# First FFN product by one level of Strassen's algorithm over 1024-token halves

## The reference

```python
    x = layer_norm(DEEPNORM_ALPHA * x + merged @ w_o, ln1_g, ln1_b)
    gate, up = jnp.split(x @ w_ffn_in, 2, axis=-1)          # (2048,1024) @ (1024, 2*2816)
    ffn = (jax.nn.silu(gate) * up) @ w_ffn_out              # (2048,2816) @ (2816,1024)
    return layer_norm(DEEPNORM_ALPHA * x + ffn, ln2_g, ln2_b)
```

## Time and profile before

| | |
|---|---|
| median of 3 runs | 1044.1 us |
| the profiled execution's own time | 1043.92 us |
| its span on the slowest core (6) | 1042.4 us |
| spans of the other cores | 1031.3 to 1039.8 us |
| TensorE busy | 1000.3 us (96%) |
| VectorE, ScalarE, GpSimd busy | 407.6, 328.0, 159.9 us |
| HBM read, written | 147.17 MB, 22.08 MB |
| mean granted TensorE clock, core 6 | 0.990 |

### The profile page before, as it was taken

The page is one execution under the profiler, slowest core; times in us unless marked ns, Lnnn a source line. Parts: engine busy times, 40 slices in busy tenths (PEclk is TensorE's granted clock), DMA queues, the critical chain, the costliest instruction groups (busy, mean ns, idle before and its releaser), DMA issues.

```text
span 1042.4 us, 15773 instructions; the slowest of 8 cores (1031.3 to 1042.4 us)
## 1 busy us (share of the span) xinstructions
PE 1000.3 (96%) x5782; PEld 466.5 (45%) x5782; DVE 407.6 (39%) x745; ACT 328.0 (31%) x472; POOL 159.9 (15%) x214
## 2 busy tenths in 40 slices
PE   4999999978999999999999999999999999999995
PEld 1455544533444444444444444444444444444442
DVE  0324576657562222222268652342124321332124
ACT  0135665746452222222225642011111111111110
POOL 3200000202244333333401320010001000000001
PEclk9999999989899999999999999999999999999998
DMA  9995145645259999800193786134421544144301
GB/s 136 176 173 103 23 91 107 82 91 78 47 83 134 139 193 141 129 1 2 46 235 134 174 220 202 41 121 149 155 81 61 177 147 142 41 141 146 117 22 60
DMA packets 40971, 118.37 MB, mean 114 GB/s; under 512 B 5120, under 2 KB 17032, under 8 KB 39648
## 3 DMA queue, kind: packets, MB, share of 16 engines
q0 software_dynamic: 13408, 49.55, 29.2%
q1 hardware_dynamic: 27488, 67.81, 22.0%
HBM read 147.17 MB, written 22.08 MB: 162 GB/s over the span
## 4 chain that ended last, share of the span: by engine, by line
PE 90%; DMA 5%; issue 1%; DVE 1%; ACT 1%; SPq 0%; POOL 0%; DVEq 0%; ACTq 0%; POOLq 0%
PE ps L231 89%; DMA arena<-w_out 2%; DMA arena<-u_scratch 2%; DMA arena<-w_glu 1%; PE ps L1068 1%; SPq L146 0%; DVE arena L1018 0%; ACT arena L595 0%; PE ps L686 0%; POOL arena L146 0%; ACT arena L643 0%; PE ps L758 0%; ACT arena L722 0%; DVE arena L1020 0%; PE ps L569 0%
## 5 line engine op out<-in xcount | busy, mean ns | idle before, releaser
L231 PE MATMUL ps<-arena 128*128 128x512 bf16 (+5 forms) x5372 | 983.5, 363 | 28.4 <-DMA arena<-xt 12.6
L231 PEld LDWEIGHTS ps<-arena 128*128 128x128 bf16 (+2 forms) x5372 | 446.4, 98 | 549.1 <-issue 71.0
L1106 DVE TENSOR_TENSOR arena<-ps,arena 128x512 bf16<-128x512 f32 x88 | 60.3, 690 | 202.4 <-PE ps L231 190.2
L827 DVE SCALAR_TENSOR_TENSOR arena<-arena,ps 128x512 f32<-128x512 f32 x96 | 65.8, 686 | 148.7 <-PE ps L231 144.7
L806 ACT ACTIVATE arena<-ps,bgate_sb 128x512 f32<-128x512 f32 x96 | 65.8, 686 | 163.3 <-PE ps L231 163.3
L1104 ACT ACTIVATE arena<-ps 128x512 f32<-128x512 f32 x88 | 52.1, 596 | 194.2 <-PE ps L231 194.2
L998 ACT ACTIVATE arena<-arena 128x1024 bf16<-128x1024 f32 (+1 forms) x32 | 33.8, 1055 | 157.7 <-DVE arena L1127 148.0
L1013 POOL TENSOR_TENSOR mvt<-mvt,eps_t 128x1 f32<-128x1 f32 x32 | 20.9, 653 | 394.9 <-DVE mvt L1008 394.8
L834 POOL TENSOR_TENSOR arena<-arena 128x512 f32<-128x512 f32 x32 | 40.7, 1273 | 123.3 <-DVE arena L827 123.3
L643 ACT ACTIVATE arena<-ps 128x1024 bf16<-128x1024 f32 x46 | 46.6, 1024 | 12.2 <-PE ps L231 11.9
L839 POOL TENSOR_TENSOR arena<-arena 128x512 bf16<-128x512 f32 x32 | 41.2, 1289 | 43.2 <-DVE arena L827 41.7
(11 more groups left out here) (90 smaller groups left out, 316.1 us busy)
## 6 DMA issues: line engine op xcount, KB each, us to landing
arena<-w_bf_cache SPq DMA_DIRECT2D x88, 512.0 KB, 3.5
arena<-u_scratch SPq DMA_DIRECT2D x64, 135.0 KB, 4.3
arena<-x SPq DMA_DIRECT2D x16, 512.0 KB, 29.5
out<-arena POOLq DMA_DIRECT2D x16, 512.0 KB, 2.9
arena<-w_f POOLq DMA_DIRECT2D x22, 256.0 KB, 7.9
arena<-w_g POOLq DMA_DIRECT2D x9, 512.0 KB, 18.9
arena<-xt POOLq DMA_DIRECT2D x8, 512.0 KB, 31.7
w_bf_cache<-w_f POOLq DMA_DIRECT2D x8, 512.0 KB, 6.2
```

The costliest lines, as they stand in the source:

```text
L231: return pe.run(lambda: nc.tensor.matmul(out, lhsT, rhs, start=start, stop=stop), deps, inc)
L827: t_y = dve.run(lambda: nc.vector.scalar_tensor_tensor(out=gb[r], in0=gb[r], scalar=1.0, in1=ps[:, bk, :], op0=ALU.add, op1=ALU.mult), [tk ...
L1106: t_a = dve.run(lambda: nc.vector.tensor_tensor(out=actT[:, j, :], in0=ps[:, bU, :], in1=sgf[sr], op=ALU.mult), [tU, t_s, e_state["dep"]])
```

## The change

`w_ffn_in` is seen as two blocks of 512 rows by 22 pairs of 128-column blocks, the input as halves of 1024 tokens, each two blocks of 512 tokens by two blocks of 512 features. Each 2x2 block product is then made with seven products in place of eight.

- *Weight forms.* Seven sums or plain blocks of the weights per unit. `fold_load`, `fold_sum` and its store make them in stage C: a load of 512 KB from the bf16 copy, three VectorE additions, a store of 896 KB to a new DRAM tensor, on SP's queue, two buffers. `straight` calls a fold after every sixth item of columns 1 to 3 (eight each, 22 in all).
- *Input forms.* `e_sums` makes five differences of x1T blocks on VectorE, at the start of each half.
- *The unit.* `f1_unit` makes four 128x512 results (two column blocks by two token blocks) of the gate or of the up part: 28 matmuls in four banks. Three products are copied out to SBUF (ScalarE), summed by GpSimd, and the later products accumulate onto the same banks; VectorE then combines bank and copy. Silu and multiply follow; two of each are put off into the next unit (`late`).
- *x and x1.* x is loaded into 12 buffers at the end of column 3, none at the start of column 1; x1 is stored to DRAM after LayerNorm 1 and loaded again for the second product (`load_hb`). `w2` takes over the buffers of x1, its 22 loads come from unit 7 on.
- *Order.* Twelve `d_chain` calls lie among the w_o blocks, eight among the units (after units 0, 1, 3, 4, 6, 7, 9, 10). The FFN goes in two halves of 1024 tokens: 11 gate units and 11 up units in turn, then eight blocks of the second product.

```diff
+    def fold_load(v):
+        if v < 22:
+            fold_ld[v] = dma(sp, FG[v % 2][:, 0:4], w1b_d[v], fg_slot[v % 2], [w1_raw[v], fold_st.get(v - 2), a_done])
...
+    def fold_sum(v):
+        G = FG[v % 2].rearrange("p s k c -> p s (k c)")
+
+        def twice(sl):
+            return bass.AP(G.tensor, G[:, sl, 0:1].offset, [[G.ap[0][0], 128], [0, 2], [1, 512]])
+
+        dve.run(lambda: nc.vector.tensor_tensor(out=G[:, 4:6, :], in0=G[:, 0:2, :], in1=twice(3), op=ALU.add), [fold_ld[v]])
+        dve.run(lambda: nc.vector.tensor_tensor(out=G[:, 6:8, :], in0=G[:, 0:2, :], in1=twice(2), op=ALU.add))
+        t = dve.run(lambda: nc.vector.tensor_tensor(out=G[:, 8, :], in0=G[:, 3, :], in1=G[:, 2, :], op=ALU.subtract))
+        fold_st[v] = dma(sp, w1f_d[v], FG[v % 2][:, 2:9], fs_slot[v % 2], [t])
+
+    fold_n = iter(range(22))
+
+    def fold_step():
+        v = next(fold_n, None)
+        if v is not None:
+            fold_load(v + 1)
+            fold_sum(v)
...
+    def straight(items, each=0):
+        for i, (_, f) in enumerate(items):
             f()
             tick()
+            if each and i % each == each - 1:
+                fold_step()
 
...
-        load_x(tb, [a_done])
     t_ln1 = load(ln1t, bass.AP(ln1_d.tensor, 0, [[0, 128], [D, 2], [1, D]]), [a_done, t_sT[3, 3]], sp)
+    fold_load(0)
     load_wg(2, [pe.tok()])
     load_wos(2, [])
     cache_w1(4)
-    straight(cat([c_main(1, tt) for tt in range(4)]))
+    straight(cat([c_main(1, tt) for tt in range(4)]), 6)
...
     load_wg(3, [pe.tok()])
     load_wos(3, [])
     t_wo = load(w_o_sb, w_o_d, [a_done])
     cache_w1(3)
-    straight(cat([c_main(2, tt) for tt in range(4)]))
+    straight(cat([c_main(2, tt) for tt in range(4)]), 6)
     dp2_done = pe.tok()
     w1_tok = {}
     s_w2 = new_slot("w2")
-    e_state = {"sgi": 0, "oi": 0}
...
+    def load_w2(j):
+        w2_tok[j] = load(w2[j], w_f2_d[:, j, :], [x1_st[j // 2 + (12 if j < 8 else 0)]])
...
+    def load_w1(u):
+        if u < 44:
+            r = u % 3
+            w1_tok[u] = dma(sp, w1s[r], w1f_d[u % 22], w1_slot[r], [w1_free[r], fold_st[u % 22]])
...
+    straight(cat([c_main(3, tt) for tt in range(4)]), 6)
     c_done = pe.tok()
-    w1_free[2] = [c_done]
...
+    def load_x(tb):
+        t_x[tb] = dma(sp, X1[tb % 12], x_d[tb * 128:(tb + 1) * 128, :], x_slot[tb % 12], x1_free.get(tb - 12, [c_done]))
+
+    for tb in range(12):
+        load_x(tb)
+        if tb in (7, 9):
+            load_w1((tb - 7) // 2)
+    x1b_free = [[g_done], [g_done], [g_done]]
...
         d_state["ln"] = t_ln
+        x1_st[tb] = dma(sp, x1_d[tb * 128:(tb + 1) * 128, :], xb, st_slot[tb % 12], [t_ln])
+        x1_free[tb] = [x1_st[tb], d_state["cb", tb]]
+        if tb + 12 < 16:
+            load_x(tb + 12)
...
+    def e_sums(P, deps):
+        q = x1T[:, P].rearrange("p h k t -> p (h k t)")
...
+        t = [t_x1T[8 * P:8 * P + 8], fold_st[20], fold_st[21], deps]
+        sa_tok[P, 4] = dve.run(lambda: nc.vector.tensor_tensor(
+            out=S[:, 4:5, :], in0=quarter(3), in1=quarter(0), op=ALU.subtract), t)
+        sa_tok[P, 2] = dve.run(lambda: nc.vector.tensor_tensor(
+            out=S[:, 2:4, :], in0=quarter(1, 2), in1=twice(0), op=ALU.subtract))
+        sa_tok[P, 0] = dve.run(lambda: nc.vector.tensor_tensor(
+            out=S[:, 0:2, :], in0=quarter(1, 2), in1=twice(3), op=ALU.subtract))
+
+    tg_free = [[c_done], [c_done]]
+    tu_free = [[]]
+    late = {"act": [], "pool": []}
...
+    def f1_unit(u):
+        P, v = u // 22, u % 22
+        i, up = v // 2, v % 2
+        n = (v // 2) % 2
+        load_w1(u + 2)
+        W = w1s[u % 3]
+        A11, A22 = x1T[:, P, 0, 0:4, :], x1T[:, P, 1, 4:8, :]
+        T3, T4, T1 = TU if up else TG[n][0:3]
+        t_free = tu_free[0] if up else tg_free[n]
+        (ba, da), (bb, db), (bc, dc), (bd, dd) = [banks.alloc(1) for _ in range(4)]
+
+        def prod(b, form, rhs, first, deps):
+            for kc in range(4):
+                tk = mm(ps[:, b, :], W[:, form, kc, :], rhs[:, kc, :], first and kc == 0, kc == 3,
+                        deps if kc == 0 else (), inc=(kc == 3), onto=not first)
+            return tk
+
+        def grab(dst, b, deps):
+            return act.run(lambda: nc.scalar.copy(dst, ps[:, b, :]), deps)
+
+        tM3 = prod(ba, 2, A11, True, [da, w1_tok[u], t_x1T[8 * P:8 * P + 8]])
+        t3 = grab(T3, ba, [tM3, t_free, sa_tok[P, 0]])
+        run_late("act")
+        tM4 = prod(bb, 5, A22, True, [db])
+        t4 = grab(T4, bb, [tM4])
+        s = pool.run(lambda: nc.gpsimd.tensor_tensor(out=T3, in0=T3, in1=T4, op=ALU.add), [t3, t4])
+        run_late("act")
+        tM1 = prod(bc, 6, SA[:, 4], True, [dc, sa_tok[P, 4]])
+        t1 = grab(T1, bc, [tM1])
+        s1 = pool.run(lambda: nc.gpsimd.tensor_tensor(out=T1, in0=T3, in1=T1, op=ALU.add), [s, t1])
+        run_late("pool", 2)
+        tM6 = prod(bd, 4, SA[:, 3], True, [dd, sa_tok[P, 2]])
+        tM5 = prod(ba, 1, SA[:, 2], False, [t3])
+        tM2 = prod(bb, 0, SA[:, 1], False, [t4, sa_tok[P, 0]])
+        tM7 = prod(bc, 3, SA[:, 0], False, [t1])
+        w1_free[u % 3] = [tM7]
+        e_state["mm"] = tM7
+
+        def dsub(dst, b, deps, op):
+            return dve.run(lambda: nc.vector.tensor_tensor(out=dst, in0=dst, in1=ps[:, b, :], op=op), deps)
+
+        g = dsub(T3, ba, [tM5, s1], ALU.subtract)
+        if not up:
+            N = TG[n][3]
+            sg12 = act.run(lambda: nc.scalar.activation(T4, ps[:, ba, :], AF.Silu), [g])
+            banks.release(ba, sg12)
+            h = dsub(T1, bb, [tM2], ALU.subtract)
+            sg21 = act.run(lambda: nc.scalar.activation(N, ps[:, bb, :], AF.Silu), [h])
+            banks.release(bb, sg21)
+        else:
+            sg12, sg21, sg22, sg11 = e_state["sg"]
+            G3, G4, G1, GN = TG[n]
+            j1, j2 = actT[2 * i], actT[2 * i + 1]
+            a_tok[2 * i + 1, 0] = dve.run(lambda: nc.vector.tensor_tensor(
+                out=j2[:, 0:512], in0=ps[:, ba, :], in1=G4, op=ALU.mult), [sg12, g, e_state["dep"]])
+            banks.release(ba, a_tok[2 * i + 1, 0])
+            h = dsub(T1, bb, [tM2], ALU.subtract)
+            a_tok[2 * i, 1] = dve.run(lambda: nc.vector.tensor_tensor(
+                out=j1[:, 512:1024], in0=ps[:, bb, :], in1=GN, op=ALU.mult), [sg21, h])
+            banks.release(bb, a_tok[2 * i, 1])
+        c22 = dsub(T1, bd, [tM6, h], ALU.add)
+        banks.release(bd, c22)
+        c11 = dsub(T3, bc, [tM7, g], ALU.add)
+        banks.release(bc, c11)
+        if not up:
+            e_state["sg"] = [sg12, sg21, None, None]
+            sg = e_state["sg"]
+
+            def silu22():
+                sg[2] = act.run(lambda: nc.scalar.activation(T1, T1, AF.Silu), [c22])
+
+            def silu11():
+                sg[3] = act.run(lambda: nc.scalar.activation(T3, T3, AF.Silu), [c11])
+            late["act"] += [silu22, silu11]
+        else:
+            sg = e_state["sg"]
+
+            def mul22():
+                a_tok[2 * i + 1, 1] = pool.run(lambda: nc.gpsimd.tensor_tensor(
+                    out=j2[:, 512:1024], in0=T1, in1=G1, op=ALU.mult), [c22, sg[2], e_state["dep"]])
+
+            def mul11():
+                a_tok[2 * i, 0] = pool.run(lambda: nc.gpsimd.tensor_tensor(
+                    out=j1[:, 0:512], in0=T3, in1=G3, op=ALU.mult), [c11, sg[3]])
+                tg_free[n] = [a_tok[2 * i, 0], a_tok[2 * i, 1]]
+                tu_free[0] = [a_tok[2 * i, 0]]
+            late["pool"] += [mul11, mul22] if v == 21 else [mul22, mul11]
+
...
+    def load_hb(tb):
+        if tb < 16:
+            r = tb % 3
+            hb_tok[tb] = dma(sp, HB[r], x1_d[tb * 128:(tb + 1) * 128, :], hb_slot[r], [x1_st[tb], hb_free[r]])
...
         d_mm(tb)
         d_H(tb)
-        if tb >= 2 and tb % 3:
+        if tb >= 2 and tb not in (5, 10):
             d_chain()
     e_start()
-    si = 0
...
-        e_step(si)
+    e_sums(0, [c_done])
+    w2_order = list(range(8, 22)) + list(range(8))
+    for u in range(22):
+        f1_unit(u)
+        if u % 3 != 2 and chain["k"] < 18:
+            d_chain()
...
+        if u >= 7:
+            for _ in range(2):
+                if w2_order:
+                    load_w2(w2_order.pop(0))
...
+    for P in range(2):
+        run_late("act", 2)
+        run_late("pool", 2)
+        if P == 0:
+            e_sums(1, [e_state["mm"]])
+            for tb in range(3):
+                load_hb(tb)
+        for tb in range(8 * P, 8 * P + 8):
+            f2_block(tb)
+        if P == 0:
+            for u in range(22, 44):
+                f1_unit(u)
     pool.wait([s.tok() for s in s_out])
     return nc, {e.name: set(e.needed) for e in engines}
 
...
```

More of the change, by code:

```diff
@@ L228, in bank2, with mm @@
         return ps[:, b:b + 2, :].rearrange("p a b -> p (a b)")
-    def mm(out, lhsT, rhs, start, stop, deps=(), inc=False):
-        return pe.run(lambda: nc.tensor.matmul(out, lhsT, rhs, start=start, stop=stop), deps, inc)
```

(53 more changed lines are left out.)

155 lines of the change are left out of this document (49 added, 106 removed).

## The result

The changed kernel takes 1133.0 us (median of 4 runs, 1130.9 to 1134.8), the kernel before 1043.0 us in the runs beside it: a ratio of 1.086, 95% interval 1.083 to 1.089. The forecast was 1126 us. All eight cores are slower by about the same (spans of 1117.6 to 1129.4 us; the stops in stage C add up to 64.0 to 68.0 us on each), so one core stands for the others.

The account below looks back on a forecast made before the run. TensorE, busy 96% of the span, was taken to bound the kernel. 1043.9 - 38.0 (matmuls) + 65 (stage C) + 8 (clock) + 9 (first unit) + 30 (chains) + 8 (turns) = 1125.9, forecast 1126 us; range 1050 to 1160.

Parts of the forecast that it names:

- Matmuls, -38.0: First FFN product: 1232 matmuls in place of 1408, 176 fewer at 0.2158 us each, saving 38.0 us.
- Stage C, 65: Merge stage: VectorE's waits for fold loads stop TensorE for 29 and 16 us in column 1, 20 in column 2.
- the walk: Step-by-step reckoning of when loads, stores and engines finish; in stage C, fold load 0 about 371 us, TensorE resuming at 374.
- w_o stage and first unit, 9: LN chains on VectorE, then e_sums and evacuations, delay the first unit's end from 578.1 to 587.4 us: 9 us.
- Chains, 30: Between units: evacuations stand behind six LN chains' casts on ScalarE, costing 3 x 4.2 + 3 x 5.9 = 30 us.
- Turns, 8: Between the two products: GpSimd's late last product, 1.8 us twice, and a second-phase weight load, 4 us; sum 8.
- the aside on VectorE and GpSimd: Second phase: VectorE and GpSimd shut each other out, so 2.3 us sums hold the last multiply back, 2 us on one turn.
- The clock, 8: Half-rate clock after four stalls, three in stage C and one at the first unit: 4 x 2.1 = 8 us.
- Rival 1: Stage C: the folds are covered, without the 65 us and three clock drops (6): 1055 us; chance 0.16.
- Rival 2: Whole kernel: only TensorE's work counts, loads and evacuations arrive before it runs dry: 1018 us, faster; chance 0.12.
- Rival 3: Stores in two packets a row, or lateness handed on between units: 1161 us; chance 0.10 together with rival 4.
- rival 4: The change doesn't do what it says, e.g. accumulating onto an evacuated bank slows TensorE; 1 in 50, priced with Rival 3.

Follow-up runs that it names:

- e8: e5's kernel with three fold buffers instead of two, fold loads two folds ahead, x1 stores behind the weight load, LN table loads moved later: 1023.3 us, ratio 0.981.
- e7: Kernel before, with one wait added: after item 6 of column 1 VectorE waits for the third x load; no fold: 1069.8 us, ratio 1.028.
- e2: Changed kernel with the DRAM-to-DRAM casts of w_ffn_in done row by row in 4 KB pieces, same bytes: 1132.4 and 1144.7 us, ratio 1.091.
- e4: Changed kernel without DRAM-to-DRAM casts: folds load straight from float32 weights on GpSimd's queue, w_o's load moved to column 3: 1090.7 us, ratio 1.045.
- e3: Changed kernel with ScalarE's cast in six LN chains issued after the next unit's third evacuation: 1121.1 us, ratio 1.075.
- e1: Changed kernel without stage C's folds; units load raw blocks, same bytes, so the result is not the reference's: 1063.2 us, ratio 1.019.
- e5: e4 with next-column weight loads dripped, LN chains after gate units only with ScalarE parts late, e_sums and output stores moved: 1048.5 us, ratio 1.007.

## Why the prediction was right, step by step

- **Matmuls, -38.0.** Right: e8 has 37.2 of it in TensorE's busy time, and the units without chains run at 0.2164 us a matmul (58.87 us for 272).
- **Stage C, 65.** The idle time is 24.5 + 17.5 + 0.5 + 22.1 + 3.5 = 68.0 us against 29 + 16 + 20. Stage C as a whole is 263.4 us long (319.65 to 583.1) against 187.4: 76, with the clock's 6 predicted 71. The steps hold too: load 0 after 42.7 us (46 predicted), store 0 in 13.7 (11), load 2 in 20.1 us (19), no stop in the rest of column 1, one long one in column 2. e7 shows the first stop without any fold, e2 that the length of the other queue's packets sets how long it is. The rule behind the walk, one packet for one packet, is only in part right: while load 2 was under way the counts were 66 and 248, so that its time fits says less than it seems. The bound of 100 us (two packets for each 7 KB row) did not come: a row went as one packet. e4 takes the casts away and gives 42 us back.
- **w_o stage and first unit, 9.** 583.1 to 658.8 is 75.7 us; the walk gave 587.4 - 511.6 = 75.8.
- **Chains, 30.** 658.80 to 754.18 is 95.4 us for ten units and seven transposes, 63.6 us of work: 31.8. Units after a gate unit wait less than those after an up unit, as predicted (2.2 to 3.2 us against 3.8 to 4.1). But the split was wrong: only 20.0 us are idle time, and 11.8 are half clock (0.88 over the window), which my walk had not priced here. I took 4.2 and 5.9 us of waiting per unit, the trace has 2.2 to 4.1. The total was right by two errors of opposite sign. e3 shows the mechanism, in part.
- **Turns, 8.** 2.48 + 4.10 + 1.62 = 8.2. But I had put the 4 us in the second phase down to the weight load, and the trace names ScalarE's evacuation: another cause than the predicted one, with the predicted size by chance. Two lines of GpSimd show what stands in front: the output store of block 7 waits for LayerNorm 2 on VectorE, and the unit's first sum, whose evacuations had ended by 905 us, is issued behind it.

```profile
908.41 0.58 POOL L148 DMA_DIRECT2D out<-arena  x1 [3.33 <-DVE arena L1054]
909.01 1.27 POOL L1179 TENSOR_TENSOR arena<-arena 128x512 f32<-128x512 f32 x1
```

  The first turn is 0.9 us longer than the last, where the aside on VectorE and GpSimd had 2: beside the sums of the second phase the late multiply took 2.1 us in place of 1.27, and the four-block sums 3.35 in place of 2.2. With these sums moved behind the first block (e5, e8) this turn is 1.6 us too.
- **The clock, 8.** Too small: stage C's stops cost about 8 us alone (6 predicted), and the 11.8 us above come on top.
- **Sum.** 1043.9 - 38.0 + 76 + 9.2 + 31.8 + 8.2 = 1131.1, against this execution's 1130.9. That it closes this well is luck. The walk starts from core 6 before, whose column 1 began at 324.2 us; on core 1 here it began at 319.75 (the cores of one execution differ by 7 to 10 us in this, in both kernels). And 3.4 us are in no term: 0.7 of waiting for a weight load and 2.7 of clock behind the stop of 4.10 us (592 matmuls in 130.44 us).
- **Rivals.** Rival 1 (folds covered) would be 1055; e1, which leaves them out, gives 1063. Rival 2 fell with it: even then the FFN's waits exceed the saving. Rival 3's two packets a row did not come, and nor did rival 4: where nothing waits, a matmul that accumulates onto an evacuated bank keeps the 0.216 us.

## What to carry to other kernels

Before a load is hung on an in-order engine, look up how long loads of that queue take in just that stretch, not how long they take in the median: here 4 us and 43 us. Price an algorithm with fewer matmuls by the lead that TensorE has over each engine that must hand something back to it within the unit, and by what stands in front of that hand-back in the engine's queue. What is not needed by the next matmul (casts, statistics, stores) goes behind what is, and prefetch is deepened until the slowest stretch is covered; in this kernel that was the way from 1133 to 1023 us.

## What the runs showed of the hardware that I had not expected

Stops of only 2.2 to 4.1 us between units cost half as much again in clock: 20.0 us idle and 11.8 us at the lower level in one window. In e4 two cores had a steady granted clock of 0.81 from 360 to 400 us without a stop, while core 3 had 1.00, and in the next run it was another pair; the slower cores then stood less (10.6 and 12.4 us against 24 to 28), so a core's stops must be read beside its clock. And cutting the casts into 4 KB rows took nearly half off the wait of the first transfer of the other queue (42.7 to 22.4 us) and left the sum of the waits nearly as it was (68.0 to 54.8 us).
